# A float32 mixture-of-experts layer: weight layout, product shape and engine assignment in the expert stage

## The chip, the core and the metric

The kernel runs on one core of a Trainium2 chip. The metric is the device time of one launch in microseconds (us), as the median over runs. TensorE (PE in the rows) multiplies, VectorE (DVE), ScalarE (ACT) and GpSimd (POOL) do elementwise work, SyncE (SP) issues most transfers, and 16 DMA engines carry them. Each engine takes its instructions strictly in the order in which they are written and waits on semaphores.

## What is computed

One encoder layer for two batches (512 and 256 tokens, 1024 columns, float32): attention and a gated linear recurrence, an output projection, a residual, and then a mixture of experts, two of 32 experts for each token. The change is about the mixture:

```python
g_logits = h @ w_rg + b_rg                       # 4 groups, the best one taken
e_logits = (h @ w_re + b_re) of that group       # 8 experts, the best two taken
for e in range(N_EXPERTS):                       # 32
    a = jax.nn.silu(h @ w_eg[e]) * (h @ w_eu[e]) # 1024 -> 256, twice
    out = out + gate[:, e:e + 1] * (a @ w_ed[e]) # 256 -> 1024
x = x + out
return rmsnorm(x, norm_final)
```

## The kernel before

The first 945 us (projections, attention, recurrence, output projection) are untouched but for one operation at their end: `norm2` (L1626) writes the normalised activations `h2`, six tiles of 128 tokens x 1024, which TensorE transposes for the router and GpSimd writes to memory (`h2_d`).

The router then gives each expert a list of up to 128 tokens. The expert stage works through 32 tiles, tile e being expert e with its tokens. Every float32 operand of a product is split into a high part (`hi_...`, rounded) and a residual (`lo_...`), and every product is three matmuls: hi by hi, hi by lo, lo by hi (`product3`, L1202 to L1204). For one tile:

- SyncE loads three weight blocks of 1 MB (`load`, L747): `raw_gate` and `raw_up`, whose source rows are 1 KB (256 columns) on the partition that holds row k * 128 + p, and `raw_down`, with rows of 4 KB. There are three buffers of each, so tile e + 3 goes where tile e was: gate and up wait for the gate/up product of tile e, down for its down product. In the same queue, after the loads of tile e + 3, stands `store(e)` (L752): it waits for `y_done` of tile e and writes `m_y`, 512 KB in rows of 4 KB. The loads of tile e + 4 stand behind it.
- ScalarE rounds each block to `hi_...` (L964). GpSimd subtracts to get `lo_gate` (L896), VectorE to get `lo_up` and `lo_down` (L1748), in place.
- GpSimd gathers the tokens' rows into `m_x` (L901), TensorE transposes them (L1365), ScalarE and VectorE make `m_xT_hi` and `m_xT_lo` (L1138, L1754).
- TensorE multiplies gate and up (`gate_up`, 2 x 24 matmuls of 256 columns into halves of one bank), ScalarE takes silu (L1146), VectorE multiplies (`m_a`, L1764), TensorE transposes the product (L1386), ScalarE and VectorE split it (L1152, L1768), and TensorE does the down product (`down`, 12 matmuls of 512 columns into two banks).
- `result` (L1776): VectorE copies the two banks to `m_y`, after which `y_done` lets the store go and frees the banks for the next down product.

The order is written by hand in a function `tile` for each engine, which is unrolled for six tiles inside a loop. In step e TensorE does gate_up(e + 1), the transposition of tile e's product, the transposition of x for tile e + 2, down(e); ScalarE does silu(e), hi of gate and up for e + 2, hi of the product of e, hi of x for e + 2, hi of down for e + 1; VectorE does the product of e, lo_up(e + 2), lo of the product of e, lo of x for e + 2, lo_down(e + 1), result(e). After the last tile the results of all pairs are gathered, added, normalised and stored.

Of the kernel before, what the change touches and what calls it, by code (L numbers as in the profile page):

```python
# [23 lines left out]
P = 128  # L24
D = 1024
# [257 lines left out]
def build(nc, A, outs):  # L283
# [9 lines left out]
    with ctx:  # L293
# [157 lines left out]
        kinds = ("gate", "up", "down")  # L451
        m_raw, m_hi, m_lo = {}, {}, {}
        for n, x in enumerate(kinds):
            shape = [2, D] if x == "down" else [KD, FF]
            m_raw[x] = at(f"raw_{x}", [P, WRING] + shape, F32, 8 + 24 * n)
            m_lo[x] = at(f"lo_{x}", [P, WRING] + shape, F32R, 8 + 24 * n)
            m_hi[x] = at(f"hi_{x}", [P, 2] + shape, F32R, 80 + 16 * n)
        m_x = at("m_x", [P, 2, D], F32, 128)
# [81 lines left out]
        LOOPED = 4  # L540
        FIRST, TURN = 2, 2 * WRING

# [116 lines left out]
        def _(sp):  # L659
# [29 lines left out]
            for s in steps:  # L689
# [35 lines left out]
                if s.kind == "ts" and s.dest == ("out", 0) and s.i == 0:  # L725

                    evac_done(sp, E_, last_pb)
                    for i in range(NT):
                        sp.dma_start(x1[:, i, :], x_rows(i)).then_inc(x1_in[i], 16)
                    sp.dma_start(g_moe[:, :], bcast(A["norm_moe"], D)).then_inc(moe_in, 16)  # L730
                    sp.dma_start(wr[:, :, 0:NGRP], A["w_router_group"][0].rearrange("(k p) n -> p k n", p=P)).then_inc(moe_in, 16)
                    sp.dma_start(wr[:, :, NGRP:NR], A["w_router_expert"][0].rearrange("(k p) n -> p k n", p=P)).then_inc(moe_in, 16)
# [3 lines left out]
            src = {"gate": A["w_exp_gate"][0].rearrange("e (k p) n -> p e k n", p=P),  # L736
                   "up": A["w_exp_up"][0].rearrange("e (k p) n -> p e k n", p=P),
                   "down": A["w_exp_down"][0].rearrange("e (k p) n -> p e k n", p=P)}
            y_rows = y_d.rearrange("(s p) n -> p s n", p=P)

            def load(expert, e, r):
                for x in kinds:
                    if not (isinstance(e, int) and e < WRING):

                        sp.wait_ge(y_mm if x == "down" else gu_mm, e - WRING + 1 if r is not None else e)
                    slot = r or 0
                    sp.dma_start(m_raw[x][:, slot], src[x][:, bass.ds(expert, 1), :, :].rearrange("p e k n -> p (e k) n"))\  # L747
                      .then_inc(w_arrived[x][slot], 16)

# [35 lines left out]
        def _(pool):  # L785
# [94 lines left out]
            for e, x in ((0, "gate"), (0, "up"), (0, "down"), (1, "gate")):  # L880
                need(pool, E_, w_hi_done[x], e + 1)
                pool.tensor_tensor(m_lo[x][:, e], m_raw[x][:, e], m_hi[x][:, e].bitcast(F32),
                                   ALU.subtract).then_inc(w_lo_done[x], 1)
                need(pool, E_, w_lo_done[x], e + 1)
# [8 lines left out]
            def lo_gate(e, p, r, copied):  # L893
                pool.wait_ge(w_hi_done["gate"], e + 1)
                pool.wait_ge(x_copied, copied)
                pool.tensor_tensor(m_lo["gate"][:, r], m_raw["gate"][:, r], m_hi["gate"][:, p].bitcast(F32),  # L896
                                   ALU.subtract).then_inc(w_lo_done["gate"], 1)
# [51 lines left out]
        def _(act):  # L949
# [10 lines left out]
            def hi_weights(x, e, p, ring, r, u):  # L960
                act.wait_ge(w_arrived[x][r], u * 16 + 16)
                if not (isinstance(e, int) and e < ring):
                    act.wait_ge(y_mm if x == "down" else gu_mm, e + (1 - ring))
                act.activation(m_hi[x][:, p], m_raw[x][:, r], ACT.Copy).then_inc(w_hi_done[x], 1)  # L964

# [203 lines left out]
            first_tiles(act.Fori, tile)  # L1169

            def beyond_tile(e, j, k, u):
# [4 lines left out]
                hi_a(e, 0, 1)  # L1176

            beyond(act, beyond_tile)
# [8 lines left out]
        def _(pe):  # L1187
# [180 lines left out]

            def gate_up(e, p, r, ring):

                pe.wait_ge(xt_lo, e + 1)
                if not (isinstance(e, int) and e < ring):
                    pe.wait_ge(a_done, e + (1 - ring))
                for n, x in enumerate(("gate", "up")):
                    pe.wait_ge(w_lo_done[x], e + 1)
                    ins = product3(psum[B_GU[p]][:, n * FF:(n + 1) * FF],
                                   [(m_xT_hi[:, p, j, :], m_xT_lo[:, p, j, :], m_hi[x][:, p, j, :], m_lo[x][:, r, j, :])
                                    for j in range(KD)])
                ins.then_inc(gu_mm, 1)

# [8 lines left out]
            def down(e, p, r):  # L1389
                pe.wait_ge(at_lo, e + 1)  # L1390
                pe.wait_ge(w_lo_done["down"], e + 1)
                if not (isinstance(e, int) and e == 0):
                    pe.wait_ge(y_done, e)
                for half in range(2):
                    cols = slice(half * 512, (half + 1) * 512)
                    ins = product3(psum[B_Y[half]][:, :],
                                   [(m_aT_hi[:, p, j, :], m_aT_lo[:, p, j, :], m_hi["down"][:, p, j, cols],
                                     m_lo["down"][:, r, j, cols]) for j in range(2)])
                ins.then_inc(y_mm, 1)
# [5 lines left out]
            xt(1, 1, 0)  # L1405
            gate_up(0, 0, 0, 2)

            def tile(e, p, k, r, u):
                if ahead(e, 1):
                    gate_up(e + 1, 1 - p, later(r, u, 1)[0], 2)  # L1410
                aT(e, p, 2)
                if ahead(e, 2):
                    xt(e + 2, p, k + 1)
                down(e, p, r)

            first_tiles(pe.Fori, tile)

            def beyond_tile(e, j, k, u):
                xt(e, 0, k)
                gate_up(e, 0, 0, 1)  # L1420
                aT(e, 0, 1)
                down(e, 0, 0)
# [5 lines left out]
        def _(dve):  # L1428
# [15 lines left out]
            for s in steps:  # L1444
# [174 lines left out]
                elif k == "norm2":  # L1619
# [126 lines left out]
            def lo_weights(x, e, p, r):  # L1746
                dve.wait_ge(w_hi_done[x], e + 1)
                dve.tensor_tensor(m_lo[x][:, r], m_raw[x][:, r], m_hi[x][:, p].bitcast(F32),  # L1748
                                  ALU.subtract).then_inc(w_lo_done[x], 1)
# [20 lines left out]

            def result(e, p, k):
                dve.wait_ge(y_mm, e + 1)
                if not (isinstance(k, int) and k == 0):
                    dve.wait_ge(y_out[p], k * 16)
                for half in range(2):
                    ins = dve.tensor_copy(m_y[:, p, half * 512:(half + 1) * 512], psum[B_Y[half]][:, :])  # L1776
                ins.then_inc(y_done, 1)

            for x in ("up", "down"):
# [17 lines left out]

            def beyond_tile(e, j, k, u):
# [4 lines left out]
                lo_a(e, 0)  # L1803
                result(e, 0, k)

# [68 lines left out]
```

## Time and profile before

| | us |
|---|---|
| three runs | 1421.17, 1424.04, 1426.96 (median 1424.04) |
| the profiled execution, first to last instruction | 1427.5 |
| start of the first expert's weight loads | 943.8 |
| first gate/up product | 1006.6 |
| end of the last `m_y` copy | 1389.3 |

The expert stage takes about 380 us of the span. The profiled execution's span is 3.5 us over the median of the runs.

The profile is read by stages. A view by windows gives the busy time of every engine, the clock granted to TensorE (1.00 is 2.4 GHz, 0.50 is 1.2 GHz), the busy share of the 16 DMA engines and what they moved. The chain of waits is followed back from the last instruction: at each step the row names what released it. A DMA row of the chain runs from issue to landing.

### The profile page before, as it was taken

Reading aid. Unit: us, or ns where it says so; the run is one execution under the profiler, and the core shown is the slowest. Engines: PE = TensorE matmul, PEld = TensorE weight load, DVE = VectorE, ACT = ScalarE, POOL = GpSimd, SP = SyncE. Lnnn points to the kernel's source line nnn. Section 1 sums busy time; section 2 is a strip of 40 time slices with the busy share of each in tenths; the row PEclk is TensorE's granted clock in tenths of the full one; section 3 lists DMA queues with packets and bytes.
Section 4 is the critical chain, followed back from the end, with each engine's and each line's share of the span. In section 5 each row is a group of like instructions: output and inputs, shape, how many; then the busy total and the mean of one; then the engine's idle time right before and its main releaser. Section 6 shows DMA issues by size and latency. Waiting matters only on the chain. (4 is left out here: it accounts for less than half of the span.)

```text
span 1427.5 us, 19757 instructions
## 1 busy us (share of the span) xinstructions
PE 1235.1 (87%) x7936; PEld 1139.9 (80%) x7936; DVE 627.7 (44%) x1051; ACT 555.8 (39%) x905; POOL 446.3 (31%) x196
## 2 busy tenths in 40 slices
PE   6989999998899888999999998971889888988870
PEld 3988999797697877999999998961778878887860
DVE  5002111227435354541121132247477777766756
ACT  6223242344454352332122130151465666566632
POOL 2211120131120201221121242233466676666613
PEclk8999999998999999999999999985898999999995
DMA  7520001233111301202212214063598999999937
GB/s 250 163 60 30 30 9 41 85 91 109 46 45 46 89 1 49 62 23 87 67 38 75 66 61 151 31 212 134 165 335 286 329 310 341 317 321 318 341 137 265
DMA packets 158728, 200.39 MB, mean 140 GB/s; under 512 B 11625, under 2 KB 139773, under 8 KB 158654
## 3 DMA queue, kind: packets, MB, share of 16 engines
q1 hardware_dynamic: 151150, 183.41, 39.3%
q0 software_dynamic: 7504, 15.94, 3.2%
q8 instruction: 53, 0.87, 0.3%
q14 instruction: 21, 0.17, 0.0%
HBM read 179.32 MB, written 34.42 MB: 150 GB/s over the span
## 5 line engine op out<-in xcount | busy, mean ns | idle before, releaser
L837 POOL TENSOR_TENSOR w_lo<-raw,w_hi 128x2048 fp32r<-128x2048 f32 (+2 forms) x37 | 152.6, 4124 | 689.5 <-ACT w_hi L975 689.4
L1202 PE MATMUL bank<-hT_hi,w_hi 128*128 128x384 f32 (+1 forms) x592 | 203.6, 344 | 4.0 <-DVE hT_lo L1491 4.0
L1203 PE MATMUL bank<-hT_lo,w_hi 128*128 128x384 f32 (+1 forms) x592 | 200.7, 339 | 0.0
L1204 PE MATMUL bank<-hT_hi,w_lo 128*128 128x384 f32 (+1 forms) x592 | 200.5, 339 | 0.0
L896 POOL TENSOR_TENSOR lo_gate<-raw_gate,hi_gate 128x2048 fp32r<-128x2048 f32 x30 | 139.2, 4641 | 121.0 <-ACT hi_gate L964 120.8
L1202 PE MATMUL bank<-w_hi,hT_hi 128*128 128x256 f32 x528 | 158.5, 300 | 0.0
L1204 PE MATMUL bank<-w_hi,hT_lo 128*128 128x256 f32 x528 | 156.6, 297 | 0.0
L1203 PE MATMUL bank<-w_lo,hT_hi 128*128 128x256 f32 x528 | 156.6, 297 | 0.0
L1748 DVE TENSOR_TENSOR lo_up<-raw_up,hi_up 128x2048 fp32r<-128x2048 f32 x31 | 109.0, 3516 | 53.6 <-ACT hi_up L964 53.5
L1202 PEld LDWEIGHTS bank<-hT_hi,w_hi 128*128 128x128 f32 (+1 forms) x592 | 111.8, 189 | 8.5 <-DVE hT_lo L1491 4.4
L975 ACT ACTIVATE w_hi<-raw 128x2048 fp32r<-128x2048 f32 (+2 forms) x42 | 74.0, 1763 | 103.7 <-PE bank L1204 103.7
L1203 PEld LDWEIGHTS bank<-hT_lo,w_hi 128*128 128x128 f32 (+1 forms) x592 | 112.0, 189 | 1.3 <-issue 0.6
L1204 PEld LDWEIGHTS bank<-hT_hi,w_lo 128*128 128x128 f32 (+1 forms) x592 | 111.6, 189 | 1.5 <-issue 0.8
L1202 PEld LDWEIGHTS bank<-w_hi,hT_hi 128*128 128x128 f32 x528 | 110.0, 208 | 2.8 <-issue 2.7
L1203 PEld LDWEIGHTS bank<-w_lo,hT_hi 128*128 128x128 f32 x528 | 110.2, 209 | 0.0
L1204 PEld LDWEIGHTS bank<-w_hi,hT_lo 128*128 128x128 f32 x528 | 110.2, 209 | 0.0
L1522 DVE CUSTOM_DVE_ANT_0 sc<-bank,table 128x128 f32<-128x128 f32 (+2 forms) x72 | 21.2, 319 | 201.5 <-PE bank L1261 201.5
L1202 PE MATMUL bank<-hi_down,m_aT_hi 128*128 128x512 f32 x128 | 60.1, 470 | 47.9 <-DVE m_aT_lo L1768 47.3
L901 POOL DMA_INDIRECT m_x<-h_d,x_idx x32 | 88.5, 2765 | 6.9 <-issue 2.7
L964 ACT ACTIVATE hi_up<-raw_up 128x2048 fp32r<-128x2048 f32 x32 | 61.3, 1916 | 40.9 <-DMA raw_up<-in_w_exp_up 40.9
L1202 PEld LDWEIGHTS bank<-hi_down,m_aT_hi 128*128 128x128 f32 x128 | 27.3, 213 | 60.7 <-DVE m_aT_lo L1768 55.5
L1748 DVE TENSOR_TENSOR lo_down<-raw_down,hi_down 128x2048 fp32r<-128x2048 f32 x31 | 70.9, 2286 | 9.5 <-ACT hi_down L964 9.5
(285 smaller groups left out, 2895.3 us busy)
## 6 DMA issues: line engine op xcount, KB each, us to landing
raw_gate<-in_w_exp_gate SPq DMA_DIRECT2D x32, 1024.0 KB, 7.7
raw_up<-in_w_exp_up SPq DMA_DIRECT2D x32, 1024.0 KB, 10.8
raw_down<-in_w_exp_down SPq DMA_DIRECT2D x32, 1024.0 KB, 6.0
raw<-in_w_in SPq DMA_DIRECT2D x25, 1024.0 KB, 6.0
y_d<-m_y SPq DMA_DIRECT2D x32, 512.0 KB
y_d<-zeros SPq DMA_DIRECT2D x11, 512.0 KB, 7.2
raw<-in_w_in SPq DMA_DIRECT2D x8, 512.0 KB, 5.9
raw<-in_w_proj_b SPq DMA_DIRECT2D x4, 1024.0 KB, 5.0
```

Source lines behind the costliest of these rows:

```text
L837: pool.tensor_tensor(w_lo[:, g % 2, 0:kb, 0:n], raw[:, g % 2, 0:kb, 0:n], w_hi[:, g % 2, 0:kb, 0:n].bitcast(F32), ALU.subtract).then_inc(w ...
L896: pool.tensor_tensor(m_lo["gate"][:, r], m_raw["gate"][:, r], m_hi["gate"][:, p].bitcast(F32), ALU.subtract).then_inc(w_lo_done["gate"], 1)
L901: pool.indirect_dma_start(m_x[:, p, :], None, h2_d, bass.IndirectOffsetOnAxis(ap=x_idx[:, p:p + 1].bitcast(U32), axis=0), bounds_check=T - ...
L964: act.activation(m_hi[x][:, p], m_raw[x][:, r], ACT.Copy).then_inc(w_hi_done[x], 1)
L975: act.activation(w_hi[:, g % 2, 0:kb, 0:n], raw[:, g % 2, 0:kb, 0:n], ACT.Copy).then_inc(whi_done, 1)
L1202: pe.matmul(out, l_hi, r_hi, start=j == 0, stop=False)
L1203: pe.matmul(out, l_hi, r_lo, start=False, stop=False)
L1204: ins = pe.matmul(out, l_lo, r_hi, start=False, stop=j == n - 1)
L1522: ins = dve.tensor_tensor_reduce(out=sc[:, u.n % 3, cols], in0=b_[:, cols], in1=bias, scale=1.0, scalar=-3e38, op0=ALU.add, op1=ALU.max, a ...
L1748: dve.tensor_tensor(m_lo[x][:, r], m_raw[x][:, r], m_hi[x][:, p].bitcast(F32), ALU.subtract).then_inc(w_lo_done[x], 1)
```

## The change

- The source of gate and up is read with input row p * 8 + k on partition p, so a partition's part of one block is one contiguous run of 8 KB, where it was 8 runs of 1 KB. The order of the contracted index changes with it: `norm2` writes `h2` with the columns permuted (it reads x1 and the norm weight with a step of 8 elements), and the router's weights are read in the same order.
- gate and up lie side by side in `hi_gu` and `lo_gu`, and one matmul of 512 columns takes both: 24 matmuls in place of 48.
- TensorE does the first half of gate_up(e + 1), then the two transpositions, then the second half, then down(e).
- `result` moves from VectorE to ScalarE, and from step e to step e + 1. VectorE's `lo_down(e + 1)` comes ahead of the lo of the product of e, and ScalarE's `hi_down(e + 1)` ahead of the hi of that product.
- Four tiles are written out ahead of the loop and four after it, in place of two and six. GpSimd's instructions stay as they are. SyncE's order stays too.

ScalarE, one step in the steady part, before:

```order
L1146 ACTIVATE m_sil<-bank 128x256
L964 ACTIVATE hi_gate<-raw_gate 128x2048
L964 ACTIVATE hi_up<-raw_up 128x2048
L1152 ACTIVATE m_aT_hi<-bank 128x256
L1138 ACTIVATE m_xT_hi<-bank 128x512 x2
L964 ACTIVATE hi_down<-raw_down 128x2048
```

ScalarE, the same step now (`hi_gu` twice is gate and up of tile e + 2):

```order
L1162 ACTIVATE m_sil<-bank 128x256
L980 ACTIVATE hi_gu<-raw_gu 128x8x256 x2
L1176 ACTIVATE m_y<-bank 128x512 x2
L980 ACTIVATE hi_down<-raw_down 128x2048
L1168 ACTIVATE m_aT_hi<-bank 128x256
L1154 ACTIVATE m_xT_hi<-bank 128x512 x2
```

The copies to `m_y`, those of tile e - 1, now stand behind the rounding of gate and up of tile e + 2. VectorE, one step, before:

```order
L1764 TENSOR_TENSOR m_a<-m_sil,bank 128x256
L1748 TENSOR_TENSOR lo_up<-raw_up,hi_up 128x2048
L1768 TENSOR_TENSOR m_aT_lo<-bank,m_aT_hi 128x256
L1754 TENSOR_TENSOR m_xT_lo<-bank,m_xT_hi 128x512 x2
L1748 TENSOR_TENSOR lo_down<-raw_down,hi_down 128x2048
L1776 COPY m_y<-bank 128x512 x2
```

VectorE, the same step now:

```order
L1801 TENSOR_TENSOR m_a<-m_sil,bank 128x256
L1785 TENSOR_TENSOR lo_gu<-raw_gu,hi_gu 128x2048
L1785 TENSOR_TENSOR lo_down<-raw_down,hi_down 128x2048
L1805 TENSOR_TENSOR m_aT_lo<-bank,m_aT_hi 128x256
L1791 TENSOR_TENSOR m_xT_lo<-bank,m_xT_hi 128x512 x2
```

The copies are gone from here, and `lo_down` stands ahead of `m_aT_lo`. The core of the diff:

```diff
+        raw_gu = at("raw_gu", [P, WRING, 2, KD, FF], F32, 8)
+        lo_gu = at("lo_gu", [P, WRING, 2, KD, FF], F32R, 8)
+        hi_gu = at("hi_gu", [P, 2, KD, 2, FF], F32R, 80)
...
-        FIRST, TURN = 2, 2 * WRING
+        FIRST, TURN = 4, 2 * WRING
...
-            src = {"gate": A["w_exp_gate"][0].rearrange("e (k p) n -> p e k n", p=P),
+            src = {"gate": A["w_exp_gate"][0].rearrange("e (p k) n -> p e (k n)", p=P),
...
# ScalarE
+            def result(e, p, k):
+                act.wait_ge(y_mm, e + 1)
+                if not (isinstance(k, int) and k == 0):
+                    act.wait_ge(y_out[p], k * 16)
+                for half in range(2):
+                    ins = act.activation(m_y[:, p, half * 512:(half + 1) * 512], psum[B_Y[half]][:, :], ACT.Copy)
+                ins.then_inc(y_done, 1)
...
                     hi_weights("up", e + 2, p, 2, *later(r, u, 2))
+                if not first(e):
+                    result(e - 1, 1 - p, k - 1 + p)
+                if ahead(e, 1) and not first(e):
+                    hi_weights("down", e + 1, 1 - p, 2, *later(r, u, 1))
                 hi_a(e, p, 2)
                 if ahead(e, 2):
                     hi_x(e + 2, p, 2)
-                if ahead(e, 1) and not first(e):
-                    hi_weights("down", e + 1, 1 - p, 2, *later(r, u, 1))
...
# TensorE
+                out = psum[B_GU[p]][:, :].rearrange("p (a n) -> p a n", a=2)
+                for j in ks:
+                    l_hi, l_lo = m_xT_hi[:, p, j, :], m_xT_lo[:, p, j, :]
+                    r_hi, r_lo = hi_gu[:, p, j, :, :], lo_gu[:, r, :, j, :]
+                    pe.matmul(out, l_hi, r_hi, start=j == 0, stop=False)
+                    pe.matmul(out, l_hi, r_lo, start=False, stop=False)
+                    ins = pe.matmul(out, l_lo, r_hi, start=False, stop=j == KD - 1)
...
                 if ahead(e, 1):
-                    gate_up(e + 1, 1 - p, later(r, u, 1)[0], 2)
+                    gate_up(e + 1, 1 - p, later(r, u, 1)[0], 2, range(0, KD // 2))
                 aT(e, p, 2)
                 if ahead(e, 2):
                     xt(e + 2, p, k + 1)
+                if ahead(e, 1):
+                    gate_up(e + 1, 1 - p, later(r, u, 1)[0], 2, range(KD // 2, KD))
                 down(e, p, r)
...
# VectorE
-                    dve.scalar_tensor_tensor(h2[:, i, :], x1[:, i, :], rstd[:, i:i + 1], g_moe[:, :],
-                                             ALU.mult, ALU.mult).then_inc(h2_done, 1)
+                    split = lambda x: x.rearrange("p (q k) -> p k q", k=KD)
+                    dve.scalar_tensor_tensor(h2[:, i, :].rearrange("p (k q) -> p k q", k=KD), split(x1[:, i, :]),
+                                             rstd[:, i:i + 1], split(g_moe[:, :]), ALU.mult, ALU.mult).then_inc(h2_done, 1)
...
                     lo_weights("up", e + 2, p, later(r, u, 2)[0])
+                if ahead(e, 1) and not first(e):
+                    lo_weights("down", e + 1, 1 - p, later(r, u, 1)[0])
                 lo_a(e, p)
                 if ahead(e, 2):
                     lo_x(e + 2, p)
-                if ahead(e, 1) and not first(e):
-                    lo_weights("down", e + 1, 1 - p, later(r, u, 1)[0])
-                result(e, p, k)
```

## Rows read from the trace of the kernel before

**Rows 1.** The page, 40 slices of the span: DMA busy share in tenths.

```profile
DMA  7520001233111301202212214063598999999937
```

**Rows 2.** Windows, steady expert stage: engines' busy us, clock, DMA share, GB/s.

```profile
1041.00:1346.00 305.00, 264.71 (x1762) 241.44 (x1760) 226.52 (x203) 185.12 (x179) 198.09 (x77) 0.94 0.94 320
```

**Rows 3.** Chain of waits, one lap of two tiles: start, duration, what.

```profile
1198.02 10.28 DMA raw_up<-in_w_exp_up
1208.32 1.92 ACT hi_up L964
1210.27 3.81 DVE lo_up L1748
...
1214.47 0.50 PE bank L1202
...
1219.73 0.69 DVE m_y L1776
...
1220.57 0.37 SPq L752
...
1221.60 11.34 DMA raw_up<-in_w_exp_up
```

**Rows 4.** Timeline of SyncE's queue: gate loads of tiles 3, 4 and 31.

```profile
1012.77 0.37 SPq L747 DMA_DIRECT2D raw_gate<-in_w_exp_gate  x1
...
1026.98 0.43 SPq L747 DMA_DIRECT2D raw_gate<-in_w_exp_gate  x1
...
1350.98 0.43 SPq L747 DMA_DIRECT2D raw_gate<-in_w_exp_gate  x1
```

**Rows 5.** L747, gate and up of tile 3 alone: issue to landing.

```profile
DMA to landing us min/median/max: 7.0/8.1/9.3
```

**Rows 6.** Page, DMA issues: one load of 1 MB alone; median us to landing.

```profile
raw<-in_w_proj_b SPq DMA_DIRECT2D x4, 1024.0 KB, 5.0
```

**Rows 7.** Chain at the end of the stage: the last store alone.

```profile
1389.28 2.61 DMA y_d<-m_y
```

**Rows 8.** Timeline of SyncE's queue: the load ahead of the x loads.

```profile
853.46 0.37 SPq L696 DMA_DIRECT2D raw<-in_w_out  x1
```

**Rows 9.** L729, the x loads with 4 KB rows: starts, issue to landing.

```profile
L729 SPq DMA_DIRECT2D x<-in_x_prompt x4: 341/432/435, 855.0 to 856.4; - x4
L729 SPq DMA_DIRECT2D x<-in_x_sample x2: 432/432/432, 856.8 to 857.3; - x2
...
DMA to landing us min/median/max: 5.2/7.3/9.3
```

**Rows 10.** Windows: rates of 4 KB rows, 1 KB rows, and a 4 KB store.

```profile
856.00:866.00 10.00, 4.66 (x20) 4.37 (x21) 6.01 (x3) 1.30 (x2) 4.41 (x1) 0.73 1.04 400
606.00:607.50 1.50, 1.50 (x15) 1.50 (x14) 0.27 (x1) 0.00 (x0) 0.00 (x0) 1.00 1.09 387
...
1390.20:1391.20 1.00, 0.00 (x0) 0.00 (x0) 0.00 (x0) 0.00 (x0) 0.00 (x0) 1.00 0.99 406
```

**Rows 11.** Groups by line and form, 1040 to 1380: busy us, mean ns, idle before.

```profile
L1748 DVE TENSOR_TENSOR lo_down<-raw_down,hi_down 128x2048 fp32r<-128x2048 f32 x29 | 66.3, 2286 | 9.0 <-ACT hi_down L964 9.0
...
L1776 DVE COPY m_y<-bank 128x512 f32<-128x512 f32 x56 | 35.9, 683 | 14.5 <-PE bank L1204 14.5
...
L1138 ACT ACTIVATE m_xT_hi<-bank 128x512 fp32r<-128x512 f32 x56 | 30.4, 595 | 12.4 <-PE bank L1365 11.5 <-issue 1.0
```

**Rows 12.** Timeline of TensorE: two matmuls of 512 columns, two of 256.

```profile
1109.12 0.39 PE L1202 MATMUL bank<-hi_down,m_aT_hi 128*128 128x512 f32 x1
...
1109.35 0.39 PE L1203 MATMUL bank<-lo_down,m_aT_hi 128*128 128x512 f32 x1
...
1112.31 0.28 PE L1202 MATMUL bank<-hi_gate,m_xT_hi 128*128 128x256 f32 x1
...
1112.43 0.28 PE L1203 MATMUL bank<-lo_gate,m_xT_hi 128*128 128x256 f32 x1
```

**Rows 13.** Line 1626, `norm2` (h in the rows is `h2`): durations, who waits.

```profile
L1626 DVE SCALAR_TENSOR_TENSOR h<-x,rstd,g_moe x6: 1283/1285/1285, 920.4 to 946.1; 128x1024 f32<-128x1024 f32 x6
...
  PE bank L1340: 1.9, 1
```

More of the change, by code:

```diff
@@ L451, in build, with raw_of, lo_of, hi_of @@
         kinds = ("gate", "up", "down")
[L452 to L457, printed above, removed]
+        SIDE = {"gate": 0, "up": 1}
+        raw_gu = at("raw_gu", [P, WRING, 2, KD, FF], F32, 8)
+        lo_gu = at("lo_gu", [P, WRING, 2, KD, FF], F32R, 8)
+        raw_down = at("raw_down", [P, WRING, 2, D], F32, 56)
+        lo_down = at("lo_down", [P, WRING, 2, D], F32R, 56)
+        hi_gu = at("hi_gu", [P, 2, KD, 2, FF], F32R, 80)
+        hi_down = at("hi_down", [P, 2, 2, D], F32R, 112)
+        def raw_of(x, r):
+            return raw_down[:, r] if x == "down" else raw_gu[:, r, SIDE[x]]
+        def lo_of(x, r):
+            return lo_down[:, r] if x == "down" else lo_gu[:, r, SIDE[x]]
+        def hi_of(x, p):
+            return hi_down[:, p] if x == "down" else hi_gu[:, p, :, SIDE[x], :]
         m_x = at("m_x", [P, 2, D], F32, 128)
@@ L746, in load @@
                     slot = r or 0
-                    sp.dma_start(m_raw[x][:, slot], src[x][:, bass.ds(expert, 1), :, :].rearrange("p e k n -> p (e k) n"))\
-                      .then_inc(w_arrived[x][slot], 16)
+                    if x == "down":
+                        sp.dma_start(raw_of(x, slot), src[x][:, bass.ds(expert, 1), :, :].rearrange("p e k n -> p (e k) n"))\
+                          .then_inc(w_arrived[x][slot], 16)
+                    else:
+                        sp.dma_start(raw_of(x, slot).rearrange("p k n -> p (k n)"),
+                                     src[x][:, bass.ds(expert, 1), :].rearrange("p e n -> p (e n)"))\
+                          .then_inc(w_arrived[x][slot], 16)
             def store(e, p):
@@ L881, in _ @@
                 need(pool, E_, w_hi_done[x], e + 1)
-                pool.tensor_tensor(m_lo[x][:, e], m_raw[x][:, e], m_hi[x][:, e].bitcast(F32),
+                pool.tensor_tensor(lo_of(x, e), raw_of(x, e), hi_of(x, e).bitcast(F32),
                                    ALU.subtract).then_inc(w_lo_done[x], 1)
@@ L895, in lo_gate @@
                 pool.wait_ge(x_copied, copied)
-                pool.tensor_tensor(m_lo["gate"][:, r], m_raw["gate"][:, r], m_hi["gate"][:, p].bitcast(F32),
+                pool.tensor_tensor(lo_of("gate", r), raw_of("gate", r), hi_of("gate", p).bitcast(F32),
                                    ALU.subtract).then_inc(w_lo_done["gate"], 1)
@@ L963, in hi_weights @@
                     act.wait_ge(y_mm if x == "down" else gu_mm, e + (1 - ring))
-                act.activation(m_hi[x][:, p], m_raw[x][:, r], ACT.Copy).then_inc(w_hi_done[x], 1)
+                act.activation(hi_of(x, p), raw_of(x, r), ACT.Copy).then_inc(w_hi_done[x], 1)
             for s in steps:
@@ L1165, in tile @@
                     hi_x(e + 2, p, 2)
-                if ahead(e, 1) and not first(e):
-                    hi_weights("down", e + 1, 1 - p, 2, *later(r, u, 1))
             first_tiles(act.Fori, tile)
+            result(NE - 1, (NE - 1) % 2, (NE - 1) // 2)
             def beyond_tile(e, j, k, u):
@@ L1176, in beyond_tile @@
                 hi_a(e, 0, 1)
+                result(e, 0, k)
             beyond(act, beyond_tile)
@@ L1367, in xt, with gate_up @@
                 ins.then_inc(xt_mm, 1)
[L1369 to L1379, printed above, removed]
+            def gate_up(e, p, r, ring, ks):
+                if ks.start == 0:
+                    pe.wait_ge(xt_lo, e + 1)
+                    if not (isinstance(e, int) and e < ring):
+                        pe.wait_ge(a_done, e + (1 - ring))
+                    for x in ("gate", "up"):
+                        pe.wait_ge(w_lo_done[x], e + 1)
+                out = psum[B_GU[p]][:, :].rearrange("p (a n) -> p a n", a=2)
[5 more added lines that the diff above has]
+                    ins = pe.matmul(out, l_lo, r_hi, start=False, stop=j == KD - 1)
+                if ks.stop == KD:
+                    ins.then_inc(gu_mm, 1)
             def aT(e, p, ring):
@@ L1396, in down @@
                     ins = product3(psum[B_Y[half]][:, :],
-                                   [(m_aT_hi[:, p, j, :], m_aT_lo[:, p, j, :], m_hi["down"][:, p, j, cols],
-                                     m_lo["down"][:, r, j, cols]) for j in range(2)])
+                                   [(m_aT_hi[:, p, j, :], m_aT_lo[:, p, j, :], hi_down[:, p, j, cols],
+                                     lo_down[:, r, j, cols]) for j in range(2)])
                 ins.then_inc(y_mm, 1)
@@ L1405, in _ @@
             xt(1, 1, 0)
-            gate_up(0, 0, 0, 2)
+            gate_up(0, 0, 0, 2, range(0, KD))
             def tile(e, p, k, r, u):
                 if ahead(e, 1):
-                    gate_up(e + 1, 1 - p, later(r, u, 1)[0], 2)
+                    gate_up(e + 1, 1 - p, later(r, u, 1)[0], 2, range(0, KD // 2))
                 aT(e, p, 2)
@@ L1419, in beyond_tile @@
                 xt(e, 0, k)
-                gate_up(e, 0, 0, 1)
+                gate_up(e, 0, 0, 1, range(0, KD))
                 aT(e, 0, 1)
@@ L1747, in lo_weights @@
                 dve.wait_ge(w_hi_done[x], e + 1)
-                dve.tensor_tensor(m_lo[x][:, r], m_raw[x][:, r], m_hi[x][:, p].bitcast(F32),
+                dve.tensor_tensor(lo_of(x, r), raw_of(x, r), hi_of(x, p).bitcast(F32),
                                   ALU.subtract).then_inc(w_lo_done[x], 1)
@@ L1769, in lo_a @@
                                   m_aT_hi[:, p, :, :].bitcast(F32), ALU.subtract).then_inc(at_lo, 1)
[L1771 to L1777, printed above, removed]
             for x in ("up", "down"):
@@ L1803, in beyond_tile @@
                 lo_a(e, 0)
-                result(e, 0, k)
             beyond(dve, beyond_tile)
```

6 lines of the change are left out of this document (3 added, 3 removed).

## The prediction, made before the changed kernel ran

> **What bounds the kernel now.** I read the page's slices first: the DMA engines are near full only from about 1035 us on [rows 1], so the change's place is the expert stage. The windows then give its steady part: TensorE is busy 265 of 305 us, DMA share 0.94 at 320 GB/s [rows 2]. Neither settles it: a queue with work in it shows 1.04 to 1.09 [rows 10], so the DMA engines have gaps too. The chain of waits decides [rows 3]. It is a closed lap: the up block of tile n lands (10.28 us after its issue), ScalarE rounds it (1.92), VectorE subtracts (3.81), only then splits the product of tile n - 2, TensorE does down(n - 2) (from 1214.47 to about 1219), VectorE copies it (ends at 1220.42), SyncE stores it and, behind the store, issues up of tile n + 2 at 1221.60. The lap is 23.6 us for **two** tiles, 11.8 for one. Over the stage, gate loads of tiles 4 and 31 are 324.0 us apart [rows 4]: 12.0 us for each of 27 steps. So the bound is a chain of latencies with one landing in two tiles, near a DMA bound.
>
> **The change part by part.**
>
> *Results on ScalarE, a step later.* This is the part that I think decides. SyncE's order is loads(n), store(n - 3), loads(n + 1). The store waits for result(n - 3), which ScalarE now does in step n - 2 behind the rounding of gate and up of tile n. So the loads of tile n + 1 can't be issued until the up block of tile n has landed and been rounded. Queued behind the waiting store are three loads, and all engines wait for those. The lap now covers **one** tile:
>
> - rounding of up: 1.92 [rows 3];
> - two copies from a bank by ScalarE: no row shows them in this form, the same shape out of a bank takes 0.595 [rows 11], so 1.19 (on VectorE 0.683 each); between ends of 1.1 and 1.4, since ScalarE's larger operations differ little;
> - a wake-up: 0.07, and from the end of the copy over store and gate issue to the up issue 1.18 (1220.42 to 1221.60) [rows 3];
> - L, from the up issue to its landing.
>
> That is 4.36 + L.
>
> *8 KB runs.* L has to be bounded, no 8 KB load is in the trace. In the lap the engines carry store 0.52 MB, gate and up 2.10 and the gathered rows about 0.2 (1536 rows of 4 KB over 32 tiles): 2.82 MB. down(n) falls ahead of them, in the time in which SyncE waits. Rates: 1 KB rows 387 GB/s, 4 KB rows 400 to 406 [rows 10]. By rate alone the change is worth 2.10 MB x (1/387 - 1/403), 0.2 us a tile. Fixed part: a 1 MB load alone takes 5.0 [rows 6], less 2.7 of moving is 2.3. The seven loads from 853.46 on (1.05 MB and six of 0.52) end at 857.3 + 9.3 = 866.6 [rows 8, 9]: 13.1 us, less 4.2 MB / 400 is 2.6. I take 2.4 from the store's issue, plus 2.82/0.400 = 7.05; the up issue stands 1.03 behind the store's (1220.57, 1221.60). L = 8.4. Upper end: the pair of 1 KB-row loads of tile 3, with an empty queue, took 9.3 from the up issue [rows 5], where the same sum gives 7.2; if 8 KB runs keep these 2 us and the store adds 0.5, L = 10.9. Lower end: the last store shows a fixed part of only 1.3 (2.61 less 0.52/0.406) [rows 7]; with that L = 7.3. I take 8.4, since the x loads are loads, in a queue, with long rows.
>
> The lap is 4.36 + 8.4 = 12.8 us a tile, against 12.0: **27 x 0.8 = +21.6 us**. The last up block lands earlier after its issue (8.4 against the usual 11): -2.6.
>
> *One product of 512 columns.* 512 columns take 0.23 us, 256 take 0.12 [rows 12]: 24 x 0.227 = 5.45 for 48 x 0.118 = 5.66, 0.2 us a tile. TensorE needs about 9.5 us a tile (5.45, 12 x 0.227, transpositions 1.3) and waits for the lap, so this counts only in the last tile: -0.2.
>
> *Halves and transpositions, `lo_down` ahead of the product's split.* lo_up ends 5.7 us after the landing of up, lo_down 2.29 later [rows 3, 11], the split 0.4: down(n - 2) can start at 8.4 and ends near 11.2 at full clock. Its copy on ScalarE comes only at the next landing plus 1.9. With a lap of 12.8 there are 3.5 us to spare, so this costs nothing here. If TensorE gets half its clock in that stretch (in the lap shown, down took 4.5 instead of 2.7), it ends at 13.9, still in time. Without that cover each us would cost half a us a tile. The stage's tail has no more weights to wait for: copies 0.2 shorter: with the above -0.9 in all.
>
> *`norm2` with a step of 8.* Six operations of 1.285 us; no row shows such a step. TensorE waited for one of them (1.9 us) [rows 13], and the last stands before the router. Ends: 0 (same speed) and 2.6 (twice the time, two of six exposed). I take 1.3. A step of 32 bytes touches a new line of memory with each element; the Trainium skill, "SBUF — State Buffer", section on the DMA port swizzle, gives 16-byte lines and a penalty for every access that crosses into a new one. By that I would go to the upper end, +1.3 more. No row here shows it.
>
> *The loop's split and the router's loads*: the same instructions in other blocks, nothing.
>
> **Sum.** +21.6 - 2.6 - 0.9 + 1.3 = +19.4. On the profiled 1427.5 that is 1447; the median of the runs is 3.5 lower, so 1424 + 19.4 = **1443.5 us**.
>
> **The rivals.**
>
> *A. The store lap as above, L from 7.9 to 9.2*: 1424 + 27 x (0.26 to 1.56) - 2.2 = 1429 to 1464. Chance 0.48.
>
> *B. The same lap, but long runs keep the pair's slow ending*: lap 14.0 to 15.3, so 1424 + 27 x 2 = 1478 and more. For it: 9.3 us for a pair alone. Against: the x loads show no such excess. Chance 0.17.
>
> *C. Faster: loads start as promptly as the store did.* L = 7.3, lap 11.7: 27 x (-0.3) - 3.7 - 0.9 + 1.3 = -11.4, 1413 us. It decides where L falls below 7.6. For it: with 128 runs in place of 1024 for a block, up to 1 us of slow start could go. Against: the fixed 2.3 to 2.6 of all loads seen, 4 KB rows among them. Chance 0.13.
>
> *D. The lap isn't closed the way I read it and the stage is simply a DMA bound*: then 2.10 MB go 0.2 to 0.4 us quicker in 28 tiles, -6 to -11, 1413 to 1418. The Trainium skill, "Perfetto Trace Analysis", section "DMA Optimizations", calls moving from 2 KB to 4 or 8 KB the primary optimization for a DMA-bound kernel, dramatic in effect; the rates of 1 KB and 4 KB rows here, 387 and 400 to 406, say a few per cent. Against D: the order of SyncE's queue is fixed and the copies do stand behind the rounding. Chance 0.07.
>
> *E. Gain and loss meet*, lap near 12.1 (L = 7.7): 1417 to 1429. Chance 0.15.
>
> A measurement of this kernel can tell about 0.5% (7 us) from no change. Slower by more than that: nearly all of A but its edge and B, 0.65; within it: E and the edges of A and D, 0.17; faster: C and most of D, 0.18. The range leaves out the far end of B and the low ends of C and D: 1414 to 1484.
>
> **What would show it.** Right: in the profile after, up loads wait for a store each time, gate issues lie 12.8 us apart, the chain reads DMA up, ACT hi, ACT `m_y`, SP, DMA up with no VectorE and no TensorE in it, and the DMA share falls from 0.94 to about 0.8. Wrong: a chain that still passes through VectorE and TensorE, or issues under 12 us apart; then L is the term that I mis-sized. `norm2` at 1.3 or 2.6 us settles its term.

## The result, and the profile after

| | before | after |
|---|---|---|
| median of the runs, us | 1424.8 | 1457.85 |
| the runs, us | 1421.17 to 1426.96 | 1457.28 to 1467.74 |
| span of the profiled execution, us | 1427.5 | 1455.8 |
| distance of gate issues, tile 4 to 31, for each of 27 steps, us | 12.00 | 13.26 |

The changed kernel is slower: the ratio is 1.024, with a 95% interval of 1.020 to 1.028, +33 us in the medians. Sign and range were right. The size was not: +19.4 forecast, +33 in the medians and +28.3 in the spans of the two profiled executions.

The page of after, in 40 slices as [rows 1] (DMA busy share in tenths), and its row for the up loads, with the median from issue to landing at the end:

```profile
DMA  7511001341130310211221150262687778787747
...
raw_gu<-in_w_exp_up SPq DMA_DIRECT2D x32, 1024.0 KB, 8.9
```

Where [rows 1] has nines, from about 1070 us on, there are sevens and eights now. The windows of the steady part answer to [rows 2]:

```profile
1041.00:1341.00 300.00, 240.58 (x1030) 191.51 (x1031) 184.09 (x139) 187.40 (x206) 201.65 (x69) 0.90 0.79 292
```

DMA share 0.94 to 0.79, 320 to 292 GB/s, and TensorE is idle for longer. No resource got tighter. The steady part waits more, as a longer chain would have it. The GB/s say this more plainly than the share, which also falls with long runs alone (0.94 to 0.86 at 321 GB/s, in an experiment below).

SyncE's queue, timeline, the gate loads that answer to tile 4 and tile 31 in [rows 4]:

```profile
1025.65 0.43 SPq L762 DMA_DIRECT2D raw_gu<-in_w_exp_gate  x1
...
1383.65 0.34 SPq L762 DMA_DIRECT2D raw_gu<-in_w_exp_gate  x1
```

358.0 us for 27 steps, 13.26 each, where [rows 4] gives 12.0. The span splits there: the stage up to tile 4 is 1.3 us earlier, the 27 steps add 34.0, and from the last gate issue to the end it is 72.15 us in place of 76.5, 4.4 less. Together 28.3. All of the loss is in the lap.

The chain of waits passes mostly through laps of two kinds, to be read against [rows 3]. The first, from one up issue to the next (start, duration, what):

```profile
1094.16 8.88 DMA raw_gu<-in_w_exp_up
...
1103.06 1.12 ACT hi_gu L980
...
1104.88 1.08 ACT m_y L1176 x2
...
1106.11 0.36 SPq L768
...
1107.09 9.23 DMA raw_gu<-in_w_exp_up
```

Landing, rounding, ScalarE's copy, store, loads, with no VectorE or TensorE: the forecast lap, 12.9 us for **one** tile. The second kind, from the same chain:

```profile
1146.02 10.76 DMA raw_gu<-in_w_exp_up
...
1156.80 1.93 ACT hi_gu L980
1158.75 3.74 DVE lo_gu L1785
...
1164.61 0.42 DVE m_aT_lo L1805
...
1165.07 0.50 PE bank L1230
...
1170.72 1.07 ACT m_y L1176 x2
...
1171.95 0.36 SPq L768
...
1172.93 8.91 DMA raw_gu<-in_w_exp_up
```

This is the path of [rows 3], through VectorE and the down product, for **two** tiles: 26.9 us. I had not put this one in the sum. Between `lo_gu` and `m_aT_lo` stands what VectorE now does first, in its timeline:

```profile
1162.41 2.28 DVE L1785 TENSOR_TENSOR lo_down<-raw_down,hi_down 128x2048 fp32r<-128x2048 f32 x1
```

Five such laps stand between 1053 and 1251 us, at 25.65 to 27.10 us, 13.15 a tile on average. Both kinds of lap occur, and either is longer than the 12.0 a tile of before.

### The profile page after: what moved, and what is told of

Its sections match the earlier page's. It is cut to its first block and busy times, and to the rows that moved or that the text cites. A ratio compares the mean times of both kernels' runs of the same rounds, so it can differ in the third digit from the quotient of the medians.

```text
span 1455.8 us, 18251 instructions
## 1 busy us (share of the span) xinstructions
PE 1236.8 (85%) x7168; PEld 1103.0 (76%) x7168; DVE 606.0 (42%) x987; ACT 585.8 (40%) x969; POOL 475.5 (33%) x196
## 5 line engine op out<-in xcount | busy, mean ns | idle before, releaser
L1785 DVE TENSOR_TENSOR lo_gu<-raw_gu,hi_gu 128x2048 fp32r<-128x2048 f32 x31 | 124.1, 4003 | 148.8 <-ACT hi_gu L980 148.8
L912 POOL TENSOR_TENSOR lo_gu<-raw_gu,hi_gu 128x2048 fp32r<-128x2048 f32 x30 | 138.1, 4605 | 128.1 <-ACT hi_gu L980 127.9
L980 ACT ACTIVATE hi_gu<-raw_gu 128x2048 fp32r<-128x2048 f32 x64 | 122.1, 1913 | 112.8 <-DMA raw_gu<-in_w_exp_gate 84.5
L1230 PE MATMUL bank<-hi_down,m_aT_hi 128*128 128x512 f32 x128 | 65.4, 511 | 73.8 <-DVE m_aT_lo L1805 73.6
L1409 PE MATMUL bank<-hi_gu,m_xT_hi 128*128 128x512 f32 x256 | 104.1, 407 | 0.0
L1410 PE MATMUL bank<-lo_gu,m_xT_hi 128*128 128x512 f32 x256 | 100.7, 393 | 0.0
L1230 PEld LDWEIGHTS bank<-hi_down,m_aT_hi 128*128 128x128 f32 x128 | 30.5, 238 | 92.4 <-DVE m_aT_lo L1805 86.2
```

The source lines that it names most:

```text
L912: pool.tensor_tensor(lo_of("gate", r), raw_of("gate", r), hi_of("gate", p).bitcast(F32), ALU.subtract).then_inc(w_lo_done["gate"], 1)
L980: act.activation(hi_of(x, p), raw_of(x, r), ACT.Copy).then_inc(w_hi_done[x], 1)
L1230: pe.matmul(out, l_hi, r_hi, start=j == 0, stop=False)
L1409: pe.matmul(out, l_hi, r_hi, start=j == 0, stop=False)
L1410: pe.matmul(out, l_hi, r_lo, start=False, stop=False)
L1785: dve.tensor_tensor(lo_of(x, r), raw_of(x, r), hi_of(x, p).bitcast(F32), ALU.subtract).then_inc(w_lo_done[x], 1)
```

## Experiments

Every number below is the median of the timed runs and the ratio to the kernel before, with its 95% interval. The kernel before was timed again beside each (medians 1426.8 to 1428.2), so a difference of two medians is good to a few us only. The distance of gate issues is taken as above. Where no other kernel is named, an edit is made to the changed kernel.

**The store one step later.** If only the copy's place behind the rounding counts, freeing the loads from the store brings the time back.

```diff
 # SyncE
                 load(e + 3)
-                store(e)
+                if e != 0: store(e - 1)
```

> The changed kernel with one edit: in SyncE's queue the store of tile e - 1, not of tile e, stands behind the loads of tile e + 3. The copy to m_y stays on ScalarE, behind the rounding. Theory (the loads wait for a store that waits for the block before them to land and be rounded, one lap a tile): the loads of tile n + 1 now wait only for the landing of tile n - 1, two pairs are in flight, and gate issues fall from 13.3 us apart to 11.5 to 12.2: 1458 - 27 x 1.1 to 1.8 = 1410 to 1428. Rival (TensorE at a lower clock, 0.90, or VectorE's order makes the lap; the store's place is not what counts): 1450 to 1460, gate issues still 13 us apart.

Measured: 1466.2 us, 1.029 [1.024, 1.034], 13.24 us a tile. A plain miss, and 6 us above the rival's range too. The chain of this kernel, one lap:

```profile
1159.99 11.17 DMA raw_gu<-in_w_exp_up
...
1173.14 4.05 DVE lo_gu L1787
...
1177.48 2.27 DVE lo_down L1787
...
1185.65 0.38 SPq L759
...
1187.20 11.51 DMA raw_gu<-in_w_exp_up
```

The store has left the chain, and the lap is 27.2 us for two tiles all the same. Its last link is the **down load** (L759), which waits for the down product and stands ahead of gate and up in SyncE's queue. So the copy's place can't be all.

**The copy back on VectorE, alone.**

```diff
 # VectorE, at the end of tile(e)
+                result(e)
 # ScalarE
-                if not first(e):
-                    result(e - 1)
```

> The changed kernel with the copies to m_y back on VectorE at the end of step e; 8 KB runs, the product of 512 columns, the halves and the new place of lo_down stay. Theory: the lap covers two tiles again and holds one landing (8.9 in place of 11 us), lo_down 2.3 us of it more: about (8.9 + 1.9 + 4.0 + 2.3 + 0.8 + 2.7 to 5.1 + 1.3 + 1.2) / 2 = 11.6 to 12.8 a tile, 1410 to 1440. Rival (the halves and the place of lo_down are what costs): 1445 to 1460.

Measured: 1460.8 us, 1.025 [1.019, 1.031], 13.12 us a tile. The same as the changed kernel, as the rival in the expectation had it. Its chain goes through `lo_down`, `m_aT_lo` and the down product in almost every lap. Taking the forecast cause away brought nothing: something else costs as much.

**8 KB runs alone, in the kernel before.** Sources and `norm2` as in the change, all else as before.

```diff
 # the kernel before, SyncE; norm2 and router weights to match
-            src = {"gate": ....rearrange("e (k p) n -> p e k n", p=P),
+            src = {"gate": ....rearrange("e (p k) n -> p e (k n)", p=P),
```

> The kernel before with the 8 KB runs alone, which brings the permuted order and the strided norm2 with it. Theory: the two-tile lap holds one landing, 2.1 us shorter (8.9 against 11.0), so 1.0 us a tile less: 1424 - 28 = 1396, and norm2 costs 1 to 2; 1395 to 1410. Rival (runs of 8 KB are worth their rate alone, 0.2 us a tile): 1417 to 1424.

Measured: 1431.5 us, 1.0005 [0.996, 1.005], 11.96 us a tile. Up lands in 9.6 us where it took 10.8, and DMA share falls from 0.94 to 0.86 at the same 321 GB/s, but the time stays. The forecast gain of 28 us isn't there. The 1.2 us of landing are given back by VectorE's residual of up. Its row on the page of before, and on the page of this kernel:

```profile
L1748 DVE TENSOR_TENSOR lo_up<-raw_up,hi_up 128x2048 fp32r<-128x2048 f32 x31 | 109.0, 3516 | 53.6 <-ACT hi_up L964 53.5
```

```profile
L1754 DVE TENSOR_TENSOR lo_up<-raw_up,hi_up 128x2048 fp32r<-128x2048 f32 x31 | 131.8, 4251 | 26.3 <-ACT hi_up L969 25.9
```

It takes 4.25 us for 3.52. `lo_down`, of the same shape, takes 2.29 in both. The timelines of the two engines tell why: from 1040 to 1380 us each of the 28 `lo_up` starts while GpSimd's `lo_gate` runs, and each ends 2.15 us after that one has ended (to 0.02 us), in this kernel, in the kernel before and in the changed one alike. So an earlier landing of up doesn't end `lo_up` earlier. What sets that end is the landing of gate, whose median is 7.4 us here and 7.7 before: 0.3 us earlier, in a lap of two tiles.

**The copy on ScalarE, a step later, alone, in the kernel before.**

```diff
 # the kernel before, ScalarE; removed from VectorE
                     hi_weights("up", e + 2)
+                if not first(e):
+                    result(e - 1)
                 hi_a(e)
```

> The kernel before with one edit: the copies to m_y go to ScalarE, one step later, behind the rounding of gate and up (and the loop is split four, 24, four). 1 KB runs, two products of 256 columns, no halves. Theory: one lap a tile of 4.4 us and a landing of 10 to 11 after the up issue: 14.4 to 15.4 a tile, 1424 + 27 x 2.4 to 3.4 = 1489 to 1516. Rival (the move is harmless, the halves or lo_down make the changed kernel slow): 1417 to 1431.

Measured: 1484.3 us, 1.042 [1.036, 1.047], 14.07 us a tile. Its chain:

```profile
1154.95 8.51 DMA raw_up<-in_w_exp_up
...
1165.30 1.08 ACT m_y L1160 x2
...
1167.63 10.00 DMA raw_up<-in_w_exp_up
```

A lap of one tile, 12.7 us here and 14.1 with the next landing (1167.63 to 1181.73): the forecast mechanism by itself, with 1 KB runs, costs 60 us, a little under the 65 to 92 expected. It is real.

**1 KB runs in the changed kernel.**

```diff
 # SyncE; norm2 and router weights back too
-            src = {"gate": ....rearrange("e (p k) n -> p e (k n)", p=P),
+            src = {"gate": ....rearrange("e (k p) n -> p e k n", p=P),
```

> The changed kernel with rows of 1 KB again and norm2 and the router as before; the rest stays. It tells what the 8 KB runs are worth where the lap of one tile holds a landing in each. From the rows: up lands 8.9 us after its issue with 8 KB runs, 9.9 with 1 KB runs under the same lap, so 27 x 1.0 us more, less 2 for norm2: 1475 to 1490. If runs are worth their rate alone (0.2 us a tile): 1460 to 1465.

Measured: 1480.7 us, 1.040 [1.034, 1.044], 14.03 us a tile, as expected. Here long runs are worth 23 us, 0.77 a tile (14.03 less 13.26). In the lap over the copy the rounding of up, by ScalarE, follows the landing at once and takes 1.9 us whatever GpSimd does, so there the landing of up counts in full.

**`hi_down` and `lo_down` ahead of the product's split, alone, in the kernel before.**

```diff
 # the kernel before, VectorE; ScalarE's hi_down and hi_a alike
+                    lo_weights("down", e + 1)
                 lo_a(e)
                 lo_x(e + 2)
-                    lo_weights("down", e + 1)
                 result(e)
```

> The kernel before with one edit: ScalarE rounds down of tile e + 1 ahead of the product of tile e, and VectorE makes lo_down ahead of the lo of that product. Copies to m_y stay on VectorE at the end of the step. Theory of two laps (beside the lap of one tile over the copy there is the old one of two tiles over lo_down, the split, the down product and the store, and each is over 13 us a tile by itself): 2.3 us more in two tiles, 27 x 1.15 = +31: 1445 to 1465. Rival (only the copy's place counts, this order costs nothing as the prediction had it): 1418 to 1430.

Measured: 1477.2 us, 1.036 [1.032, 1.040], 13.51 us a tile. More than expected, from the edit that I had priced at nothing. The chain, one lap of two tiles:

```profile
1164.04 11.64 DMA raw_up<-in_w_exp_up
...
1177.66 4.13 DVE lo_up L1748
1181.80 2.20 DVE lo_down L1748
...
1184.39 0.80 PE bank L1202
...
1190.01 0.69 DVE m_y L1776
...
1191.88 11.11 DMA raw_up<-in_w_exp_up
```

27.8 us against 23.6 in [rows 3]: `lo_down` is now a link (2.20) and the landing is 1.4 longer (11.64 for 10.28; the medians over the stage are 11.3 and 10.8). The product takes 4.9 us, most of its matmuls 0.43 apart where [rows 12] show 0.23; in the lap of [rows 3] it took about 4.5.

**That order undone in the changed kernel**, with the copies still on ScalarE.

```diff
 # VectorE; ScalarE's hi_down and hi_a alike
-                    lo_weights("down", e + 1)
                 lo_a(e)
                 lo_x(e + 2)
+                    lo_weights("down", e + 1)
```

> The changed kernel with one of its two orders undone: the rounding of down and lo_down go back behind the product's split, and the copies stay on ScalarE behind the rounding of gate and up. If the lap of one tile over the copy carries most of the loss by itself: still 13 us apart, 1445 to 1460. If it was only the lap over lo_down: back to 1405 to 1430.

Measured: 1443.6 us, 1.014 [1.009, 1.020], 12.69 us a tile; 14 us less than the changed kernel. Its chain, one lap of the forecast kind:

```profile
1154.11 8.35 DMA raw_gu<-in_w_exp_up
...
1164.30 1.08 ACT m_y L1176 x2
...
1166.51 8.28 DMA raw_gu<-in_w_exp_up
```

12.4 us for one tile, with landings of 8.35 and 8.28. The lap over the down product is gone, and the forecast lap has nearly the forecast's size. But about half of this chain goes a third way, over GpSimd. From one gate issue to an up issue two tiles on:

```profile
1178.41 6.19 DMA raw_gu<-in_w_exp_gate
...
1186.71 4.58 POOL lo_gu L912
...
1191.43 8.98 DMA m_x<-h_d,x_idx
...
1203.89 7.76 DMA raw_gu<-in_w_exp_up
```

GpSimd issues the gather of the tokens' rows only behind its residual of gate, the rows land 9 us later, then come the transposition and the gate/up product, which frees the buffers. From up issue to up issue (1178.84 to 1203.89) that is 25.05 us for two tiles, 12.5 for one: the same length as the forecast lap. The prediction had no such lap.

**Both undone**: the copy on VectorE and the late `lo_down`; 8 KB runs, 512 columns and halves stay.

```diff
 # VectorE (ScalarE alike, without result)
-                    lo_weights("down", e + 1)
                 lo_a(e)
                 lo_x(e + 2)
+                    lo_weights("down", e + 1)
+                result(e)
```

> The changed kernel with both undone: copies on VectorE at the end of step e, and the rounding and residual of down behind the product's split, as before. 8 KB runs, one product of 512 columns and the halves stay. Theory of two laps: back to the lap of before, gate issues 11.6 to 12.2 us apart, 1412 to 1430. Rival (halves or the 512-column product cost something themselves): 1440 and more.

Measured: 1410.7 us, 0.990 [0.986, 0.994], 11.26 us a tile. Just below the 1412 to 1430 expected, and faster than before by about 1%. The four kernels with all else as in the change:

| | copy on VectorE | copy on ScalarE |
|---|---|---|
| `lo_down` behind the split | 1410.7 | 1443.6 |
| `lo_down` ahead of it | 1460.8 | 1457.85 (the change) |

From 1410.7 either edit alone adds 33 or 50 us, both together 47. They don't add up. The chains say why: each edit closes a lap of its own, and only the longer one counts.

**The halves taken out of the last kernel.** gate_up(e + 1) in one piece ahead of the transpositions, all else as there.

```diff
-                    gate_up(e + 1, range(0, KD // 2))
+                    gate_up(e + 1, range(0, KD))
                 aT(e)
                 xt(e + 2)
-                    gate_up(e + 1, range(KD // 2, KD))
```

> The kernel with the copies on VectorE and down late (1411 us) with one more edit undone: the gate/up product in one piece ahead of the transpositions. It is then the kernel before with 8 KB runs and the product of 512 columns. The kernel before with 8 KB runs alone stood at 1431. If the 20 us between them come from the halves (the transposed x and the transposed product arrive earlier on ScalarE, which then reaches down sooner): 1425 to 1435. If they come from the product of 512 columns (0.2 us a tile): 1405 to 1415, and then more than its own time was gained. Half of each: 1415 to 1425.

Measured: 1424.2 us, 0.998 [0.994, 1.001], 11.87 us a tile. So the halves carry the gain of the kernel with both undone: 13.6 us by the medians (1424.2 less 1410.7), 11 us by the ratios, whose intervals just touch at 0.994. Beside the kernel with 8 KB runs alone (ratio 1.0005) this one adds the 512-column product, and the two intervals overlap: that product alone, with the loop's other split, shows no gain.

**SyncE's order changed in the changed kernel**: gate and up of e + 3, then down of e + 2, then the store of e - 1. Neither the store nor the down load then stands ahead of gate and up with a fresh wait.

```diff
 # SyncE
-                load(e + 3, ("gate", "up", "down"))
-                store(e)
+                load(e + 3, ("gate", "up"))
+                load(e + 2, ("down",))
+                if e != 0: store(e - 1)
```

> The changed kernel with SyncE's queue written anew and nothing else: in step e it loads gate and up of e + 3, then down of e + 2, then stores tile e - 1. Gate and up of the next tile no longer stand behind the down load that waits for the down product of the step, nor behind the copy of that step, so both laps get one tile more. Theory of two laps: the issue distance falls to 10.3 to 11.6 us, near what TensorE (9.5 to 10.5) and the transfers (3.87 MB at 400 GB/s, 9.7) need: 1380 to 1415. Rival (VectorE's and ScalarE's order, not SyncE's queue, sets the pace): 1450 to 1465.

Measured: 1405.9 us, 0.987 [0.982, 0.992], 11.30 us a tile, DMA share 0.92 at 340 GB/s. Its chain between 1040 and 1340 us holds no landing of gate, up or down. With the same programs on all other engines, the queue's order alone makes 52 us.

**Queue order and the late `lo_down`**, with the copy on ScalarE, then with the copy on VectorE.

```diff
 # as above, SyncE, and VectorE:
-                    lo_weights("down", e + 1)
                 lo_a(e)
                 lo_x(e + 2)
+                    lo_weights("down", e + 1)
```

> The same kernel (down late, copies on ScalarE) with SyncE's new queue order, gate and up ahead of down and store. Theory: both laps are gone, what is left is VectorE's and TensorE's own work and the transfers, 10.5 to 11.3 us apart: 1385 to 1405. If the queue order alone had taken all there is: 1400 to 1410, as without it.

> As the last, with the copies back on VectorE at the end of the step. Theory: VectorE has 1.4 us more in each tile and waits for the down product of the step in its own queue, so it is slower than the one before it by up to 0.5 us a tile: 1390 to 1415.

Measured: 1405.4 us, 0.985 [0.981, 0.990] with ScalarE, and 1402.2 us, 0.985 [0.979, 0.990] with VectorE, the fastest median of all (11.21 us a tile). The first missed its range (1385 to 1405) by a hair, and the second wasn't slower than the first. The three kernels with this queue order can't be told apart by their intervals: once the queue no longer closes the laps, where the copy and `lo_down` stand shows nothing. Nor can they be told from the kernel at 1410.7, which has the old queue order and both edits undone. What is next, from the chain of the kernel at 1402.2:

```profile
1147.13 4.62 POOL lo_gu L916
...
1151.89 10.04 DMA m_x<-h_d,x_idx
...
1161.97 1.11 PE bank L1385 x8
...
1166.14 1.94 ACT hi_gu L984
...
1168.24 4.62 POOL lo_gu L916
```

GpSimd's residual stands ahead of its gather, whose rows take 10 us: 21.1 us for two tiles. It is the way of the third lap above. The queue has no part in it here; it closes through ScalarE's order.

## Why the prediction was right in sign and short in size

**The bound, and what was closed.** Right: a chain of latencies through SyncE's in-order queue, with the time growing. The DMA share of 0.79 hit the forecast of about 0.8 partly by luck: from 320 to 292 GB/s it would be 0.86, and the rest comes with the long runs, which the forecast of the share didn't name. Of the prediction's own signs, the forecast lap is in the chain, but so is the sign of being wrong, a chain through VectorE and TensorE. The issues are 13.26 apart, not 12.8.

**The copy lap.** Right. Forecast 12.8 us for one tile with L = 8.4; in the kernel with `lo_down` late it is 12.4 with L = 8.3. That kernel's distance is 12.69 a tile and its time 1443.6 us, which is the number forecast for the change. Some of that is luck, since the lap over the gather, which I didn't have, is as long there. The fixed part of the lap was 4.36 in the sum and 4.05 in the rows (12.93 less 8.88).

**"Halves and transpositions, `lo_down` ahead of the product's split", "so this costs nothing here".** This is the step that failed. I asked whether the down product ends before ScalarE comes to the copy, which leaves 3.5 us, or 0.8 at half clock (14.7 less 13.9). I did not close the lap over that product with a landing of its own, and did not ask what else waits for it. SyncE's down load does, and it stands in the queue ahead of store, gate and up. By the same numbers the lap over the down product was 13.9 + 0.07 + 1.19 + 1.18 + 8.4 = 24.7 for two tiles, 12.4 for one: 0.4 under the lap that I took, which is nearer than the terms are known. Measured, the way from landing to the next up issue is 16.15 (1156.78 to 1172.93; 16.3 by that sum), and the landing is what was mis-sized: 10.76, not 8.4. Here too the end of VectorE's residual hangs on gate and GpSimd: `lo_gu` of gate starts there at 1155.76 and runs 4.58 us, `lo_gu` of up starts at 1158.75, runs 3.74 and ends 2.15 after it. So this lap goes by the landing of gate. By these times up could have landed 1.4 us later without a change in it.

**Why the landing is longer.** I had written that down falls ahead, in the time in which SyncE waits. SyncE's timeline of after, just ahead of the long landing:

```profile
1142.42 0.39 SPq L759 DMA_DIRECT2D raw_down<-in_w_exp_down  x1
...
1146.02 0.80 SPq L762 DMA_DIRECT2D raw_gu<-in_w_exp_up  x1
```

And the same queue in the kernel with `lo_down` late:

```profile
1161.09 0.38 SPq L759 DMA_DIRECT2D raw_down<-in_w_exp_down  x1
...
1166.51 0.67 SPq L762 DMA_DIRECT2D raw_gu<-in_w_exp_up  x1
```

Down is 3.6 us ahead of up in the first and 5.4 in the second, where up lands in 8.28. Over the up landings that the chain of after passes through from 1053 to 1384 us: with down less than 4 us ahead, nine landings, mean 9.75 (8.91 to 10.76); with down over 5 us ahead, five, mean 8.12 (7.38 to 8.88). Over all up loads of after in that stretch, on the chain or not, the means are 9.63 (13 loads) and 8.15 (12 loads), with one load between, and in the kernel with `lo_down` late, where down is at least 5 us ahead each time, the mean is 8.4. A late down product thus seems to put part of 1 MB into the landing of up, in either kind of lap. It isn't all: with both edits undone down is 2.2 to 3.6 us ahead each time, and up lands in anything from 8.2 to 12.5. No run moved the down load by itself. The undone order took back 14 us of the 33, and the same order alone in the kernel before cost 52.

**The other terms.** The end of the stage was forecast at -2.6 - 0.9 and measured at -4.4. The product of 512 columns shows nothing alone, as forecast. The halves I priced at nothing too; where the copies and the early `lo_down` don't hide it they bring 11 to 14 us. `norm2`, which answers to [rows 13]:

```profile
L1663 DVE SCALAR_TENSOR_TENSOR h<-x,rstd,g_moe x6: 2055/2226/2304, 919.0 to 943.9; 128x1024 f32<-128x1024 f32 x6
...
  PE bank L1368: 2.7, 1
```

2226 ns for 1285, 1.73 times as long. TensorE's wait for one of them grew from 1.9 to 2.7 us. Two of them exposed would be 1.9 us, between the 1.3 taken and the upper end of 2.6, but the stage up to tile 4 was 1.3 us earlier all the same. The Trainium skill, "SBUF — State Buffer", section on the DMA port swizzle, has the direction (a penalty for each access that enters a new 16-byte line); the row gives the size, and it is less than twice.

**The rivals.** A had one of the laps, and its range (to 1464) the time. That the time fell there owes something to a lap that A didn't have: with A's lap and without the one over the down product the time is 1443.6, 14 us less. B, a lap of 14 us and more with a slow ending of the pair, is out: with `lo_down` late up lands in 8.3. D, a mere DMA bound, is out: share and GB/s fell while the time grew. On the Trainium skill's rule there ("Perfetto Trace Analysis", section "DMA Optimizations", larger transfers as the primary optimization): 8 KB for 1 KB runs was worth 23 us in the changed kernel, and nothing measurable in the kernel before. C and E are out: they wanted up to land in 7.3 or 7.7 us, and its median is 8.9.

**What stays open.** TensorE's granted clock is 0.90 in the steady part, 0.94 before and 0.96 with both edits undone. In the laps over the down product its matmuls are mostly 0.43 us apart, the level of 1.2 GHz, right after it had waited for `m_aT_lo`. At 0.23 the product would be some 2 us shorter, 1 us a tile. No run changed the clock alone, so how much of the loss is that is not known. Nor did a run move GpSimd's residual or its gather, so what those two cost in each kernel is read from chains only.

## What to carry to other kernels

When an edit delays an operation, list **everything** that waits for it, DMA issues above all, and close each lap through the in-order queue with its own landing: two laps within half a microsecond of each other must both be priced. In a queue that mixes loads and stores, put what has been free for longest first; here that order alone was worth 52 us in the changed kernel. And price a landing by what was put into the queue in the few microseconds ahead of it, not by its bytes alone. Where an operation's time varies from tile to tile (here 2.6 to 5.1 us for one shape), look what runs beside it before taking it as a fixed term.

## What the hardware showed unexpectedly

A pair of 1 MB loads with 8 KB runs lands earlier than one with 1 KB runs, by more than the rates of [rows 10] say: the median for up is 9.6 us for 10.8 in the kernel before with only that edit, where 0.2 us was worked out. What remains in the landing follows the queue in part: about 1.6 us between down just ahead and down well ahead, in the changed kernel.

A copy of 128 x 1 integers on GpSimd, which nobody had touched, became seven times as long. Its line in after, and the same line before (min/median/max in ns):

```profile
L907 POOL COPY x_idx<-slot_idx x32: 183/1327/2103, 989.0 to 1372.7; 128x1 int32 x24, 128x1 int32<-128x1 int32 x8
```

```profile
L891 POOL COPY x_idx<-slot_idx x32: 177/197/2100, 991.5 to 1346.1; 128x1 int32 x24, 128x1 int32<-128x1 int32 x8
```

One of these copies, in GpSimd's timeline of after:

```profile
1163.40 1.33 POOL L907 COPY x_idx<-slot_idx 128x1 int32 x1
```

It ends at 1164.73, and the `lo_down` shown above (1162.41, 2.28 us) at 1164.69. So it is with all 26 copies between 1040 and 1380 us: each starts while `lo_down` runs and ends 0.04 to 0.05 us after it. In the kernel with `lo_down` late each stands beside `m_xT_lo`, which has one input in a bank, and takes 0.19 to 0.20 us; with the new queue order it is a median of 1324 ns with `lo_down` early and 197 with it late. So the order of VectorE's instructions is shown to be the cause.

The other way round it is the finding of the kernel with 8 KB runs alone: VectorE's residual of up, with both inputs in on-chip memory, ends 2.15 us after GpSimd's residual of gate, in all 28 instructions of each of three kernels. Neither wait stands in a row as idle time; the instruction is recorded as longer. The Trainium skill, "SBUF — State Buffer", section "Terms", lets VectorE and GpSimd share a pair of ports to the on-chip memory, on which the loser is blocked for the whole of the other's instruction; both traces agree with it.
